# GpSimd takes half of the hidden-tile exchange, and VectorE's order around it is changed, in a two-layer decoder trunk

## The chip, the cores and the metric

The kernel runs on one core of one Trainium2 chip, all arithmetic in float32 (matmuls on split operands, below). The metric is the device time of one execution in microseconds. Three runs of the kernel before gave 2172.32, 2172.74 and 2172.97 us; the median is 2172.74 us.

## What is computed

A trunk of two layers over 256 tokens with 2048 features. Layer 0 mixes with a recurrent unit and dilated attention, layer 1 with differential attention; each mixer is followed by a layer norm, then by an MLP with a squared ReLU (2048 to 8192 to 2048) and a second layer norm. The change touches the MLPs alone, so the mixers are left out here.

```python
D_MODEL = 2048; SEQ = 256; DEPTH = 2; D_FF = 4 * D_MODEL

def layer_norm(x, g, b):
    xf = x.astype(jnp.float32)
    mu = jnp.mean(xf, axis=-1, keepdims=True)
    var = jnp.mean(jnp.square(xf - mu), axis=-1, keepdims=True)
    y = (xf - mu) * lax.rsqrt(var + LN_EPS) * g.astype(jnp.float32) + b.astype(jnp.float32)
    return y.astype(x.dtype)

def squared_relu_mlp(x, w1, w2):
    h = jax.nn.relu(x @ w1)
    return (h * h) @ w2

def reference(x, positions, ev_w_in, ev_conv_w, ev_conv_b, ev_gate_a_w, ev_gate_a_b, ev_gate_x_w,
              ev_gate_x_b, ev_rg_lambda, ev_w_out, od_w_in, od_lambda_q1, od_lambda_k1, od_lambda_q2,
              od_lambda_k2, od_subln_g, od_w_out, ln_mix_g, ln_mix_b, ln_mlp_g, ln_mlp_b, mlp_w1, mlp_w2):
    cos, sin = rope_tables(positions)
    for layer in range(DEPTH):
        p = layer // 2
        if layer % 2 == 0:
            mix = even_mixer(x, cos, sin, ev_w_in[p], ev_conv_w[p], ev_conv_b[p], ev_gate_a_w[p], ev_gate_a_b[p],
                             ev_gate_x_w[p], ev_gate_x_b[p], ev_rg_lambda[p], ev_w_out[p])
        else:
            lambda_init = 0.8 - 0.6 * math.exp(-0.3 * layer)
            mix = odd_mixer(x, cos, sin, od_w_in[p], od_lambda_q1[p], od_lambda_k1[p], od_lambda_q2[p],
                            od_lambda_k2[p], od_subln_g[p], od_w_out[p], lambda_init)
        x = layer_norm(ALPHA * x + mix, ln_mix_g[layer], ln_mix_b[layer])
        x = layer_norm(ALPHA * x + squared_relu_mlp(x, mlp_w1[layer], mlp_w2[layer]), ln_mlp_g[layer], ln_mlp_b[layer])
    return x
```

## The kernel before

**Split operands.** Each float32 weight chunk is loaded into `raw`, ScalarE copies it rounded into `w_hi` (`split_hi`), and VectorE writes the rest into `w_lo` (`split_lo`, L1005). The activations are split in the same way. A product is three matmuls: hi by hi, hi by lo, lo by hi (L714 to L716). A chunk is 2 x 128 rows by 512 columns of a weight, and a natural chunk is 12 matmuls of 128x512. Eight chunks are one block. `raw` has eight places, loaded in pairs by SP; `w_hi` and `w_lo` have four, so ScalarE splits chunk k when TensorE has used chunk k - 4.

**The MLP.** It is worked in 16 blocks of 512 hidden features (`FB`). For each there is an "up" block of eight chunks (x times w1 into PSUM banks 0 and 1) and a "down" block of eight chunks (hidden times w2 into banks 4 to 7, added into `res`). The up block of the first 512 features stands in `lead`; then iteration i of `up_down` does the up block i + 1 and the down block i: 16 chunks. On VectorE and ScalarE an iteration is the loop `for k in range(2, 18)`: chunk k of 2 to 7 belongs to the up block, 8 to 15 to the down block, and 16 and 17 to the next iteration. Chunks 0 and 1 are split in the iteration before. Iteration 0 (`first=True` on VectorE) and iteration 14 (`last=True`) are written out, 1 to 13 are a hardware loop. The down block of the last 512 features follows.

**The exchange.** The up product has tokens on partitions, the down product needs hidden features there. VectorE transposes the 32x32 squares out of PSUM into `cross` (`blocks_turned`, L1403, at k = 9), and 16 DMAs then move whole squares between the four groups of 32 partitions, from `cross` (`tiles_turned`) to `ks` (`tiles_moved`), 32 KB each (`move_hidden`, L301, on SP's queue). SP issues them behind the load of the first pair of the down block (`down`, L304) and ahead of its other pairs. Then VectorE takes the squared ReLU from `ks` into `qs` (`squared`, L1410, at k = 4), ScalarE copies its rounded part into `yT` (`hidden_hi`, L587, at k = 5), and VectorE writes the rest (`hidden_lo`, L1416, at k = 5). TensorE waits for `hidden_lo` ahead of the down block. In iteration 14 the exchange of the last block follows its transpose at once: a second `squared` comes at k = 12 and a second `hidden_lo` at k = 13.

**Other work of VectorE there.** `add_down` (L1077) adds the four down products into the residual at k = 11, 13, 15 and 17. In iteration 0 alone, `gain_residual` (L1068 and L1071) multiplies the residual by gain and ALPHA and adds the bias, one of four column groups at k = 6, 8, 12 and 14. `add_down` of a group waits for its scaling.

**GpSimd** issues the loads of gain and bias for the four layer norms (L359). Each waits until the four scalings with the values before have been made (`s_gained`). At the end it works on parts of the last layer norm. SP, GpSimd and the engines run their own instructions in order; a wait blocks all that is behind it on that engine.

Of the kernel before, what the change touches and what calls it, by code (L numbers as in the profile page):

```python
# [69 lines left out]
FB = D_FF // CN  # L70
# [74 lines left out]
def build(nc, x, positions, ev_w_in, ev_conv_w, ev_conv_b, ev_gate_a_w, ev_gate_a_b, ev_gate_x_w,  # L145
# [11 lines left out]
    with ExitStack() as ctx:  # L157
# [3 lines left out]
        def sem(name):  # L161
# [73 lines left out]
        s_bn, s_k8, s_var, s_std, s_shift = (  # L235
            sem("block_statistics"), sem("softplus_made"), sem("variance"),
            sem("std"), sem("shift"))
        s_block_tr, s_moved = sem("hidden_blocks_turned"), sem("hidden_blocks_moved")
        s_sq, s_hhi, s_hlo = sem("hidden_squared"), sem("hidden_hi"), sem("hidden_lo")
        s_S, s_neg, s_exp, s_P, s_T, s_pT, s_O = (sem("scores"), sem("neg_max"), sem("exps"), sem("probs"),  # L240
                                                  sem("probs_turned"), sem("probs_turned_copied"),
# [26 lines left out]
        @block.sync  # L268
        def _(sp):
            def load(blk, q, src):  # L270

                sp.wait_ge(s_lo, (blk - 1) * BLK + (2 * q + 2))
                sp.dma_start(raw[:, 2 * q:2 * q + 2].rearrange("p k t c -> p (k t) c"), src).then_inc(s_raw[q], 16)

            xv = x[0].rearrange("(t p) n -> p t n", p=P)
            sp.dma_start(cst[:, 0:P], consts[:, 0:P]).then_inc(s_id, 16)
            for k in range(BLK):
                cols = slice(k * CK * P, (k + 1) * CK * P)
                sp.dma_start(res[:, :, cols], xv[:, :, cols]).then_inc(s_x[k], 16)
                first = w_ein[k // 2, EVEN_IN_COLS[0]][:, k % 2 * CK:k % 2 * CK + CK]  # L280
                sp.dma_start(raw[:, k], first).then_inc(s_first[k], 16)
            sp.dma_start(cst[:, P:K_W], consts[:, P:K_W]).then_inc(s_cst, 16)
            for b, col in enumerate(EVEN_IN_COLS[1:], 1):
                for q in range(PAIRS):
                    load(B_EIN + b, q, w_ein[q, col])

            def load_out(order, blk, w):
                for n, (nb, kp, _, _) in enumerate(order[::2]):
                    load(blk + n // PAIRS, n % PAIRS, w[kp // 2, nb])

            def mlp(layer, b0):
                def up(blk, b):
                    for q in range(PAIRS):
                        load(blk, q, w_m1[layer][q, b])

                def move_hidden(b):

                    sp.wait_ge(s_block_tr, b + (layer * FB + 1))
                    for a in range(NQ):
                        for c in range(NQ):  # L300
                            sp.dma_start(tiles_moved[QUAD * c:QUAD * c + QUAD, :, a],  # L301
                                         tiles_turned[QUAD * a:QUAD * a + QUAD, c]).then_inc(s_moved, 16)

                def down(blk, b):  # L304
                    for q in range(PAIRS):
                        load(blk, q, w_m2[layer][b, q])
                        if q == 0:
                            move_hidden(b)
                up(b0, 0)
                with sp.Fori(0, FB - 1) as i:  # L310
                    up(i * 2 + (b0 + 1), i + 1)
                    down(i * 2 + (b0 + 2), i)
                down(b0 + 2 * FB - 1, FB - 1)

            load_out(EVEN_OUT, B_EOUT, w_eout)
            mlp(0, B_M0)
            with sp.Fori(0, GROUPS) as g:
                for j in range(3):
                    for q in range(PAIRS):
                        load(g * 3 + (B_OIN + j), q, w_oin[q, g + j * (D // CN)])  # L320
            load_out(ODD_OUT, B_OOUT, w_oout)
            mlp(1, B_M1)
            ov = out[0].rearrange("(t p) n -> p t n", p=P)
            dve_1, dve_2, dve_3 = ((s_fin_dve, n + 1, *piece) for n, piece in enumerate(FIN_DVE))
            pool_1, pool_2, pool_3 = ((s_fin_pool, n + 1, *piece) for n, piece in enumerate(FIN_POOL))
            stores = (dve_1, pool_1, pool_2, dve_2, pool_3, dve_3)
            for ready, count, tok, a, b in stores:
                sp.wait_ge(ready, count)
                sp.dma_start(ov[:, tok, a:b], res[:, tok, a:b]).then_inc(s_out, 16)
            sp.wait_ge(s_out, 16 * len(stores))  # L330
# [3 lines left out]
        def _(pool):  # L334
# [15 lines left out]
                    pool.dma_start(gates_w[64 * half:64 * half + 64, n, :, 64 * half:64 * half + 64], src).then_inc(s_gw, 16)  # L350


            for n in range(4):
                if n == 0:
                    pool.wait_ge(s_yalo, 2)
                else:
                    pool.wait_ge(s_gained, GROUPS * n)
                for i, row in enumerate(ln_rows(n)):
                    pool.dma_start(gain_bias[:, i], row.partition_broadcast(P)[:, 0, :]).then_inc(s_gb, 16)  # L359
            pool.wait_ge(s_gb, 128)  # L360

            for n, (tok, a, b) in enumerate(FIN_POOL):
# [8 lines left out]
        def _(act):  # L371
# [209 lines left out]
            def mlp(n, b0):  # L581

                def hidden_hi(b, dst=hT):
                    act.wait_ge(s_sq, b + 1)
                    if dst is hT:
                        act.wait_ge(s_used, last_down(b))
                    nc.scalar.activation(dst[:, :, 0].rearrange("p f (n i) -> p f n i", i=QUAD), hidden,  # L587
                                         ACT.Copy).then_inc(s_hhi, 1)

                h0 = FB * (n // 2)  # L590
                def last_down(b):
                    return ((b - h0) * 2 + b0 + 1) * BLK
                lead(n + 1, b0)

                def up_down(i, last=False):

                    blk = i * 2 + (b0 + 1)
                    for k in range(2, 18):
                        split_hi(blk, k)
                        if k == 5:  # L600
                            hidden_hi(i + h0)
                        if k == 13 and last:
                            hidden_hi(i + h0 + 1, hT_last)

                with act.Fori(0, FB - 2) as i:
                    up_down(i)
                up_down(FB - 2, last=True)
                last = b0 + 2 * FB - 1
                for k in range(2, BLK):
                    split_hi(last, k)  # L610
                if last + 1 < B_END:
                    split_hi(last + 1, 0)
                    split_hi(last + 1, 1)
                layer_norm(n + 1)
# [384 lines left out]
        def _(dve):  # L999
# [397 lines left out]
            def mlp(n, b0, n0):  # L1397
# [8 lines left out]

                def squared(b):

                    dve.wait_ge(s_moved, (b + (h0 + 1)) * (16 * NQ * NQ))
                    nc.vector.scalar_tensor_tensor(out=flat(qs[:]), in0=flat(ks[:]), scalar=0.0, in1=flat(ks[:]),  # L1410
                                                   op0=ALU.max, op1=ALU.mult).then_inc(s_sq, 1)

# [12 lines left out]
                def up_down(i, last=False, first=False):  # L1425

                    blk = i * 2 + (b0 + 1)
                    for k in range(2, 18):
                        split_lo(blk, k)
                        if k == 4:  # L1430
                            squared(i)
                        if k == 5:
                            hidden_lo(i)
                        if k == 9:
                            blocks_turned(blk, 0)
                        if first and k in (6, 8, 12, 14):
                            gain_residual(n, (6, 8, 12, 14).index(k))
                        if k == 12 and last:
                            squared(i + 1)
                        if k == 13 and last:  # L1440
# [142 lines left out]
```

## Time and profile before

| | before |
|---|---|
| median of 3 runs | 2172.74 us (2172.32 to 2172.97) |
| the profiled execution | 2174.45 us |
| span of its profile | 2172.3 us |
| mean granted TensorE clock | 0.997 of full speed |
| first MLP, up and down blocks | about 350 to 1060 us |
| second MLP | about 1450 to 2160 us |
| VectorE, ScalarE busy | 65%, 45% of the span |
| GpSimd busy | 1% of the span |
| DMA engines | 59.5% of the 16 engines' span by SP's queue, 1.3% by GpSimd's |

The profile is one execution. "Busy" counts instructions on an engine; matmuls are pipelined, so a record is drawn longer than the step from one to the next. A wait is the idle time of an engine ahead of an instruction, put down to what released it last. A DMA issue is the time the issuing queue spends on it; its landing is counted from the start of the issue. Instructions of one kind that follow each other are shown as one row with their number behind an x.

### The profile page before, as it was taken

How to read it: one execution, taken by the hardware profiler on the slowest of the kernel's cores; microseconds unless marked ns; L12 is line 12 of the kernel's file. 1: busy time of each engine (PE TensorE's matmuls, PEld its weight loads, DVE VectorE, ACT ScalarE, POOL GpSimd, SP SyncE). 2: the span in 40 equal slices, each digit the busy share in tenths (PEclk: the TensorE clock that was granted, in tenths of full speed). 3: DMA queues.
4: the chain of work that ended last, by engine and by line, in shares of the span. 5: the costliest groups of instructions: out<-in, count | busy, mean ns of one | idle time of the engine just before them, and what ended most of it. 6: DMA issues, size and time to landing. Idle time of an engine off the chain costs nothing.

```text
span 2172.3 us, 27393 instructions
## 1 busy us (share of the span) xinstructions
PE 2135.4 (98%) x10034; PEld 1786.2 (82%) x10034; DVE 1418.1 (65%) x1448; ACT 983.6 (45%) x1160; POOL 28.5 (1%) x38
## 2 busy tenths in 40 slices
PE   8999999999999999999999999999999999999996
PEld 7888888788888888887888888887888888888885
DVE  5766766666656665666787666567666666666657
ACT  4445656344434444444645545554444444444442
POOL 2000000000000000000000000000000000000002
PEclk9999999999999999999999999999999999999999
DMA  8555565666666666665564555555766666666662
GB/s 279 175 175 158 178 241 161 211 217 209 203 192 215 211 203 192 212 213 190 180 214 157 191 173 174 175 164 179 244 207 210 203 201 206 210 201 203 206 207 103
DMA packets 244768, 425.83 MB, mean 196 GB/s; under 512 B 14993, under 2 KB 50049, under 8 KB 243697
## 3 DMA queue, kind: packets, MB, share of 16 engines
q1 hardware_dynamic: 242880, 415.75, 59.5%
q0 software_dynamic: 1840, 9.44, 1.3%
q8 instruction: 31, 0.51, 0.1%
q14 instruction: 17, 0.13, 0.0%
HBM read 406.26 MB, written 2.10 MB: 188 GB/s over the span
## 4 chain that ended last, share of the span: by engine, by line
PE 91%; DVE 4%; SPq 3%; DMA 1%; issue 1%; ACT 0%; DVEq 0%
PE ps L714 24%; PE ps L716 24%; PE ps L715 24%; PE ps L688 10%; PE ps L692 5%; SPq L301 3%; DVE w_lo L1005 1%; DMA raw<-in_ev_w_in 1%; DMA ks<-cross 1%; PE ps L789 0%; DVE res L1077 0%; PE ps L754 0%; PE ps L830 0%; DVE res L1068 0%; PE ps L734 0%
## 5 line engine op out<-in xcount | busy, mean ns | idle before, releaser
L380 ACT ACTIVATE w_hi<-raw 128x1024 fp32r<-128x1024 f32 x752 | 786.5, 1058 | 808.7 <-PE ps L716 747.9
L1005 DVE TENSOR_TENSOR w_lo<-raw,w_hi 128x1024 fp32r<-128x1024 f32 x752 | 895.5, 1217 | 163.9 <-ACT w_hi L380 163.6
L714 PE MATMUL ps<-w_hi,yT 128*128 128x512 f32 x1240 | 484.3, 391 | 4.1 <-DVE w_lo L1005 4.1
L714 PE MATMUL ps<-w_hi,xT 128*128 128x512 f32 x1216 | 476.4, 392 | 7.1 <-DVE w_lo L1005 4.9
L716 PE MATMUL ps<-w_hi,yT 128*128 128x512 f32 x1240 | 482.5, 389 | 0.0
L715 PE MATMUL ps<-w_lo,yT 128*128 128x512 f32 x1240 | 482.5, 389 | 0.0
L716 PE MATMUL ps<-w_hi,xT 128*128 128x512 f32 x1216 | 474.0, 390 | 0.0
L715 PE MATMUL ps<-w_lo,xT 128*128 128x512 f32 x1216 | 473.9, 390 | 0.0
L1077 DVE TENSOR_TENSOR res<-ps,res 128x1024 f32<-128x1024 f32 x131 | 160.3, 1223 | 219.3 <-PE ps L716 219.3
L714 PEld LDWEIGHTS ps<-w_hi,yT 128*128 128x128 f32 x1240 | 232.7, 188 | 53.9 <-DVE w_lo L1005 5.8
L714 PEld LDWEIGHTS ps<-w_hi,xT 128*128 128x128 f32 x1216 | 228.7, 188 | 56.8 <-DVE w_lo L1005 7.2
L716 PEld LDWEIGHTS ps<-w_hi,yT 128*128 128x128 f32 x1240 | 232.7, 188 | 48.4
L715 PEld LDWEIGHTS ps<-w_lo,yT 128*128 128x128 f32 x1240 | 232.8, 188 | 48.2
L716 PEld LDWEIGHTS ps<-w_hi,xT 128*128 128x128 f32 x1216 | 228.6, 188 | 47.9
L715 PEld LDWEIGHTS ps<-w_lo,xT 128*128 128x128 f32 x1216 | 228.7, 188 | 47.1
L688 PE MATMUL ps<-xT,w_hi 128*128 128x512 f32 x1024 | 261.9, 397 | 1.8 <-DVE xT L1035 1.5
L688 PEld LDWEIGHTS ps<-xT,w_hi 128*128 128x128 f32 x1024 | 185.0, 189 | 36.6 <-DVE xT L1035 2.0
L1410 DVE SCALAR_TENSOR_TENSOR qs<-ks 128x1024 f32<-128x1024 f32 x32 | 39.2, 1225 | 172.5 <-DMA ks<-cross 172.5
L692 PEld LDWEIGHTS ps<-xT,w_lo 128*128 128x128 f32 x1024 | 137.4, 190 | 9.6 <-DVE xT L1035 1.1
L692 PE MATMUL ps<-xT,w_lo 128*128 128x256 f32 x1024 | 143.7, 284 | 0.9 <-DVE xT L1035 0.9
L587 ACT ACTIVATE yT<-qs 128x1024 fp32r<-128x1024 f32 x32 | 34.0, 1061 | 171.5 <-DVE qs L1410 171.5
L1403 DVE STREAM_TRANSPOSE cross<-ps 128x1024 f32<-128x1024 f32 x32 | 40.0, 1249 | 92.7 <-PE ps L716 92.7
(181 smaller groups left out, 781.1 us busy)
## 6 DMA issues: line engine op xcount, KB each, us to landing
raw<-in_mlp_w SPq DMA_DIRECT2D x256, 1024.0 KB, 5.2
raw<-in_od_w_in SPq DMA_DIRECT2D x48, 1024.0 KB, 5.2
raw<-in_ev_w_in SPq DMA_DIRECT2D x36, 1024.0 KB, 5.1
raw<-in_ev_w_out SPq DMA_DIRECT2D x16, 1024.0 KB, 5.1
ks<-cross SPq DMA_DIRECT2D x512, 32.0 KB, 1.9
raw<-in_od_w_out SPq DMA_DIRECT2D x16, 1024.0 KB, 5.1
raw<-in_ev_w_in SPq DMA_DIRECT2D x8, 512.0 KB, 12.4
res<-in_x SPq DMA_DIRECT2D x8, 256.0 KB, 9.3
```

The source lines that it names most:

```text
L301: sp.dma_start(tiles_moved[QUAD * c:QUAD * c + QUAD, :, a], tiles_turned[QUAD * a:QUAD * a + QUAD, c]).then_inc(s_moved, 16)
L380: nc.scalar.activation(flat(w_hi[:, k % NSPL]), flat(raw[:, k % NRAW]), ACT.Copy).then_inc(s_hi, 1)
L587: nc.scalar.activation(dst[:, :, 0].rearrange("p f (n i) -> p f n i", i=QUAD), hidden, ACT.Copy).then_inc(s_hhi, 1)
L688: return nc.tensor.matmul(ps[:, f], w_hi[:, k % NSPL, i, f * P:f * P + P], both, start=k == 0 and i == 0, stop=k == BLK - 1 and i == CK - 1)
L692: return nc.tensor.matmul(ps[:, f, S:2 * S], w_lo[:, k % NSPL, i, f * P:f * P + P], xT[:, CK * k + i, 0], start=False, stop=False)
L714: nc.tensor.matmul(bank, src[:, kt + i, 0, toks], hi, start=(start and i == 0), stop=False)
L715: nc.tensor.matmul(bank, src[:, kt + i, 0, toks], lo, start=False, stop=False)
L716: ins = nc.tensor.matmul(bank, src[:, kt + i, 1, toks], hi, start=False, stop=(stop and i == CK - 1))
L1005: nc.vector.tensor_tensor(flat(w_lo[:, k % NSPL]), flat(raw[:, k % NRAW]), flat(w_hi[:, k % NSPL]).bitcast(F32), ALU.subtract).then_inc(s_ ...
L1077: nc.vector.tensor_tensor(res[:, :, nb * CN:nb * CN + CN], ps[:, pair[0]:pair[0] + 2], res[:, :, nb * CN:nb * CN + CN], ALU.add).then_inc( ...
L1403: nc.vector.transpose(tiles_turned.rearrange("p c t f i -> p (t f) c i"), ps[:, bank:bank + 2].rearrange("p t (f c j) -> p (t f) c j", c=N ...
L1410: nc.vector.scalar_tensor_tensor(out=flat(qs[:]), in0=flat(ks[:]), scalar=0.0, in1=flat(ks[:]), op0=ALU.max, op1=ALU.mult).then_inc(s_sq, 1)
```

## The change

Three edits. On GpSimd a function `move_hidden` is added: it waits for the transpose and issues the DMAs of the source groups a = 2 and 3, 8 of the 16, with a semaphore of their own; SP keeps a = 0 and 1. GpSimd does block 0 of an MLP behind the load of the mixer norm's gain and bias, and blocks 1 to 15 behind the load of the MLP norm's. `squared` waits for both semaphores. VectorE squares behind chunk 6 instead of 4 and writes the hidden tile's low part behind 7 instead of 5, ScalarE its high part behind 7 instead of 5. In iteration 0 the four scalings of the residual stand behind chunks 2, 3, 10 and 12 instead of 6, 8, 12 and 14.

```diff
--- before.py
+++ after.py
@@ -235,7 +235,8 @@
         s_bn, s_k8, s_var, s_std, s_shift = (
             sem("block_statistics"), sem("softplus_made"), sem("variance"),
             sem("std"), sem("shift"))
-        s_block_tr, s_moved = sem("hidden_blocks_turned"), sem("hidden_blocks_moved")
+        s_block_tr, s_moved, s_moved_pool = (sem("hidden_blocks_turned"), sem("hidden_blocks_moved"),
+                                          sem("hidden_blocks_moved_by_gpsimd"))
         s_sq, s_hhi, s_hlo = sem("hidden_squared"), sem("hidden_hi"), sem("hidden_lo")
         s_S, s_neg, s_exp, s_P, s_T, s_pT, s_O = (sem("scores"), sem("neg_max"), sem("exps"), sem("probs"),
                                                   sem("probs_turned"), sem("probs_turned_copied"),
@@ -296,7 +297,7 @@
                 def move_hidden(b):
 
                     sp.wait_ge(s_block_tr, b + (layer * FB + 1))
-                    for a in range(NQ):
+                    for a in range(NQ // 2):
                         for c in range(NQ):
                             sp.dma_start(tiles_moved[QUAD * c:QUAD * c + QUAD, :, a],
                                          tiles_turned[QUAD * a:QUAD * a + QUAD, c]).then_inc(s_moved, 16)
@@ -350,6 +351,14 @@
                     pool.dma_start(gates_w[64 * half:64 * half + 64, n, :, 64 * half:64 * half + 64], src).then_inc(s_gw, 16)
 
 
+            def move_hidden(count):
+
+                pool.wait_ge(s_block_tr, count)
+                for a in range(NQ // 2, NQ):
+                    for c in range(NQ):
+                        pool.dma_start(tiles_moved[QUAD * c:QUAD * c + QUAD, :, a],
+                                       tiles_turned[QUAD * a:QUAD * a + QUAD, c]).then_inc(s_moved_pool, 16)
+
             for n in range(4):
                 if n == 0:
                     pool.wait_ge(s_yalo, 2)
@@ -357,6 +366,11 @@
                     pool.wait_ge(s_gained, GROUPS * n)
                 for i, row in enumerate(ln_rows(n)):
                     pool.dma_start(gain_bias[:, i], row.partition_broadcast(P)[:, 0, :]).then_inc(s_gb, 16)
+                if n % 2 == 0:
+                    move_hidden(n // 2 * FB + 1)
+                else:
+                    for b in range(1, FB):
+                        move_hidden(b + (n // 2 * FB + 1))
             pool.wait_ge(s_gb, 128)
 
             for n, (tok, a, b) in enumerate(FIN_POOL):
@@ -597,7 +611,7 @@
                     blk = i * 2 + (b0 + 1)
                     for k in range(2, 18):
                         split_hi(blk, k)
-                        if k == 5:
+                        if k == 7:
                             hidden_hi(i + h0)
                         if k == 13 and last:
                             hidden_hi(i + h0 + 1, hT_last)
@@ -1406,7 +1420,8 @@
 
                 def squared(b):
 
-                    dve.wait_ge(s_moved, (b + (h0 + 1)) * (16 * NQ * NQ))
+                    dve.wait_ge(s_moved, (b + (h0 + 1)) * (8 * NQ * NQ))
+                    dve.wait_ge(s_moved_pool, (b + (h0 + 1)) * (8 * NQ * NQ))
                     nc.vector.scalar_tensor_tensor(out=flat(qs[:]), in0=flat(ks[:]), scalar=0.0, in1=flat(ks[:]),
                                                    op0=ALU.max, op1=ALU.mult).then_inc(s_sq, 1)
 
@@ -1427,14 +1442,14 @@
                     blk = i * 2 + (b0 + 1)
                     for k in range(2, 18):
                         split_lo(blk, k)
-                        if k == 4:
+                        if k == 6:
                             squared(i)
-                        if k == 5:
+                        if k == 7:
                             hidden_lo(i)
                         if k == 9:
                             blocks_turned(blk, 0)
-                        if first and k in (6, 8, 12, 14):
-                            gain_residual(n, (6, 8, 12, 14).index(k))
+                        if first and k in (2, 3, 10, 12):
+                            gain_residual(n, (2, 3, 10, 12).index(k))
                         if k == 12 and last:
                             squared(i + 1)
                         if k == 13 and last:
```

## Rows read from the trace of the kernel before

**Rows 1.** The page's first part: busy us of each engine, share, count.

```profile
PE 2135.4 (98%) x10034; PEld 1786.2 (82%) x10034; DVE 1418.1 (65%) x1448; ACT 983.6 (45%) x1160; POOL 28.5 (1%) x38
```

**Rows 2.** TensorE's waits, windows 340:480, 1000:1080, 1440:1560, 2090:2173: total, times, longest.

```profile
PE ps L714 <- DVE w_lo L1005: 3.0, 2, 2.8
...
PE ps L714 <- DVE w_lo L1005: 2.1, 2, 1.6
...
PE ps L714 <- DVE w_lo L1005: 1.9, 2, 1.6
...
PE ps L714 <- DVE w_lo L1005: 2.0, 2, 1.6
```

**Rows 3.** VectorE in order of time, middle iterations: start us, us, line, tiles, [idle before].

```profile
522.67 1.23 DVE L1410 SCALAR_TENSOR_TENSOR qs<-ks 128x1024 f32<-128x1024 f32 x1 [5.08 <-DMA ks<-cross]
...
534.31 1.25 DVE L1403 STREAM_TRANSPOSE cross<-ps 128x1024 f32<-128x1024 f32 x1 [3.12 <-PE ps L716]
...
577.83 1.25 DVE L1403 STREAM_TRANSPOSE cross<-ps 128x1024 f32<-128x1024 f32 x1 [3.12 <-PE ps L716]
```

**Rows 4.** TensorE in order of time, at two of its waits.

```profile
393.15 0.50 PE L714 MATMUL ps<-w_hi,xT 128*128 128x512 f32 x1 [2.82 <-DVE w_lo L1005]
...
397.13 0.39 PE L715 MATMUL ps<-w_lo,xT 128*128 128x512 f32 x1
...
1498.42 0.39 PE L716 MATMUL ps<-w_hi,xT 128*128 128x512 f32 x1
...
1498.94 0.50 PE L714 MATMUL ps<-w_hi,xT 128*128 128x512 f32 x1
```

**Rows 5.** The windows view, 394 to 398 us: busy us, PEclk, DMA share, GB/s.

```profile
394.00:398.00 4.00, 4.00 (x13) 3.17 (x12) 3.97 (x5) 2.11 (x4) 0.00 (x0) 0.63 0.79 275
```

**Rows 6.** VectorE in order of time, first iteration of the first MLP.

```profile
376.77 1.25 DVE L1403 STREAM_TRANSPOSE cross<-ps 128x1024 f32<-128x1024 f32 x1 [3.06 <-PE ps L716]
...
380.59 1.23 DVE L1005 TENSOR_TENSOR w_lo<-raw,w_hi 128x1024 fp32r<-128x1024 f32 x1 [0.32 <-ACT w_hi L380]
...
390.74 1.22 DVE L1410 SCALAR_TENSOR_TENSOR qs<-ks 128x1024 f32<-128x1024 f32 x1 [8.93 <-DMA ks<-cross]
...
416.81 1.22 DVE L1068 SCALAR_TENSOR_TENSOR res<-res,rg 128x1024 f32<-128x1024 f32 x1
...
418.06 1.23 DVE L1071 SCALAR_TENSOR_TENSOR res<-rg,res 128x1024 f32<-128x1024 f32 x1
```

**Rows 7.** SP's queue in order of time, issues of three exchanges.

```profile
378.05 11.43 SPq L301 DMA_DIRECT2D ks<-cross  x16
...
424.40 10.28 SPq L301 DMA_DIRECT2D ks<-cross  x16
...
1014.30 10.19 SPq L301 DMA_DIRECT2D ks<-cross  x16
```

**Rows 8.** The chain of work, last iteration: start us, us, what.

```profile
1023.90 1.87 DMA ks<-cross
```

**Rows 9.** VectorE in order of time, last iteration of the first MLP.

```profile
1013.02 1.25 DVE L1403 STREAM_TRANSPOSE cross<-ps 128x1024 f32<-128x1024 f32 x1 [3.06 <-PE ps L716]
...
1025.80 1.22 DVE L1410 SCALAR_TENSOR_TENSOR qs<-ks 128x1024 f32<-128x1024 f32 x1 [4.97 <-DMA ks<-cross]
...
1028.14 1.23 DVE L1416 TENSOR_TENSOR yT<-qs,yT 128x1024 fp32r<-128x1024 f32 x1
```

**Rows 10.** GpSimd in order of time: two DMA issues.

```profile
1.26 0.71 POOL L335 DMA_DIRECT2D rg<-in_positions  x1 [0.80 <-POOLq L1574]
...
419.58 0.53 POOL L359 DMA_DIRECT2D rg<-in_ln_mlp_g  x1 [124.60 <-DVE res L1071]
```

**Rows 11.** DMA issues from GpSimd: count, KB each, median us to landing.

```profile
late<-in_ev_gate_x_w POOLq DMA_DIRECT2D x2, 128.0 KB, 10.0
...
rg<-in_positions POOLq DMA_DIRECT2D x1, 32.0 KB, 3.5
...
rg<-in_ev_conv_w POOLq DMA_DIRECT2D x1, 16.0 KB, 5.1
```

## The prediction

> **What bounds the kernel now.** I read the busy shares first [rows 1]: TensorE is busy for 2135.4 of the span's 2172.3 us, so only what makes TensorE wait can be won. Next I read its waits, window by window [rows 2]. All of its waiting for split weights, 9.0 us, lies in four places, two waits in each: the first two iterations and the last iteration of `up_down` in the first MLP (3.0 and 2.1 us) and in the second (1.9 and 2.0 us). The 12 iterations between them in each MLP have none.
>
> A wait costs more than its bracket. One matmul of 128x512 starts every 0.227 us: one iteration is 192 of them and two transposes of successive iterations start at 534.31 and 577.83, so 43.52 / 192 [rows 3]. A record is drawn 0.39 us long, so the bracket leaves out 0.16 us, and the first matmul behind a wait lasts 0.50 instead of 0.39 [rows 4]. Each of the eight waits therefore costs its bracket and 0.27 us. In the first MLP the longest one does more. The granted clock falls: it is 0.63 on average from 394 to 398 us [rows 5], where matmuls run at 1.2 GHz for a while instead of 2.4. From 393.15 to 397.13 there are ten steps in 3.98 us instead of 2.27 [rows 4]; 0.11 of that is in my 0.27, so the clock takes 1.6 us. Finally the matmul at 1498.94 is 0.50 long with no bracket, so a wait too short to be listed: 0.4 us by the starts.
> Sum: 9.0 + 8 x 0.27 + 1.6 + 0.4 = **13.2 us**. Early iterations: (3.0 + 1.9) + 4 x 0.27 + 1.6 + 0.4 = 8.0. Last iterations: (2.1 + 2.0) + 4 x 0.27 = 5.2.
>
> **Why TensorE waits there.** In the first iteration VectorE splits chunk 4 at 380.59 and then stands in `squared`, waiting for the exchange, until 390.74 [rows 6]. Chunk k of the iteration is due at 376.77 + 2.72 k (12 matmuls a chunk; the transpose at 376.77 marks the end of the block before), so chunk 5 at 390.4, but it is split only behind `squared`, by 390.74 + 2 x 1.22 = 393.2. The exchange is 16 transfers that SP issues one behind the other in 11.43 us, or 10.19 us where there is no hiccup, so 0.64 us each [rows 7], and the last lands 1.87 us after its issue begins [rows 8]. The issuing is the long part, not the transfers. In the last iteration the second `squared` has the same shape: transpose at 1013.02, exchange landed at 1025.8, hidden_lo at 1028.14 [rows 9]. In a middle iteration SP issues before the iteration starts, and `squared` at 522.67 makes nobody late [rows 3].
>
> **The change, part by part.**
> *Order on VectorE and ScalarE.* `squared` goes from behind chunk 4 to behind chunk 6, the hi and lo of the hidden tile from behind 5 to behind 7. Nothing is added. What becomes late next: chunk 7, due at 376.77 + 19.04 = 395.8. `squared` and its split take 2 x 1.22, so the exchange may land as late as 393.4, 15.4 us after the transpose ended; even SP alone landed at 390.7. Chunk 8, due at 398.5, follows hidden_lo: 389.1 + 4 x 1.23 = 394, or 395.7 if the exchange landed at 390.7. So the order alone removes the wait of the first iteration, if the splits ahead of `squared` are in time. The small one of the second iteration goes too: its exchange is issued from 424.40 [rows 7] and lands by 436.5, and chunk 7 is due there at 420.3 + 19.0 = 439.3.
> They now share VectorE with two residual scalings (behind 2 and 3), each two instructions, 2.48 us from 416.81 to 419.29 [rows 6]. From 378.0: chunk 2 at 379.2, scaling 381.7, chunk 3 at 382.9 (due 384.9), scaling 385.4, chunk 4 at 386.6 (due 387.7), 5 at 387.8 (due 390.4), 6 at 389.1 (due 393.1). The least margin is 1.0 us. Second half, from the transpose that ends at 399.8: 10, scaling, 11 by 404.7 (due 406.7), an addition, 12 by 407.2 (due 409.4), scaling, 13 by 410.9 (due 412.1), an addition, 14 by 413.3 (due 414.9). No wait: **-8.0 us**. Before, four scalings fell in the backlog behind the late `squared`.
> *GpSimd takes 8 of the 16 transfers.* SP's 8 are issued in 5.1 instead of 10.2 us: last iteration 1014.3 + 7 x 0.64 + 1.9 = 1020.7. GpSimd waits for the transpose itself. It reacts in about 0.3 us (the scaling that releases it ends at 419.29, it issues at 419.58), and its issue takes 0.53 us, 0.71 where it moved 32 KB to 32 partitions [rows 10]. So the last issue begins at 1014.3 + 0.3 + 7 x 0.53 = 1018.3. The trace has no such transfer from GpSimd's queue. From below its landing is SP's own 1.9 us; from above 5.1 us (16 KB) and 10.0 us (gate weights), both while SP's first loads kept the DMA engines full [rows 11]. I take 3.5 us, the 32 KB transfer that was issued first of all, as the engines are nearly idle here too. Landed: 1021.8 (1020.2 to 1028.3), against 1025.8 now. Chunk 13 is due at 1013.0 + 5 x 2.72 = 1026.6; with `squared` and the split the exchange may land at 1024.2. Chunk 14, due at 1029.3, comes behind `squared`, split, hidden_lo, addition and split, 6 us: 1023.3. Both hold up to a landing of 5 us: **-5.2 us**.
> *Other things that the edit touches.* VectorE gets a second wait in `squared`, nothing where the engine idles there. SP's loads behind the exchange are issued 5 us earlier; they gate nobody now. On GpSimd the exchanges of blocks 1 to 15 stand behind the reload of gain and bias, which waits for the fourth scaling (409.6) and takes two issues; block 1's half is then issued by 415.3, and SP's half of it only begins at about 424. In middle iterations GpSimd issues right behind the transpose, and `squared` comes some 30 us later (534.31 to 522.67 + 43.52). `squared` on one queue's 8 transfers still waits for SP, whose half begins just before the iteration.
> Sum: -13.2 us against this execution's 2174.45 us (span 2172.3) gives 2161.2. The median of the runs is 1.7 us lower, 2172.74, so **2159.5 us**.
>
> *A rule against it.* The rows show 10.2 us of issuing for 512 KB and 1.9 us of landing [rows 7, 8]. The Trainium skill, DMA: Bandwidth & Descriptors, section Issuing engines are not separate DMA queues, says that several issuers only save the sequencer's issue time, usually small beside the DMA. Read as "does not help", it would leave the 5.2 us of the last iterations in place; the trace speaks for the reverse here, as issue time is five times the landing.
>
> **The rivals.**
> 1. *GpSimd's half lands as late as SP's whole did.* That takes a landing of 7.5 us: 14.3 + 0.3 + 3.7 + 7.5 = 25.8. For it: 5.1 and 10.0 us in [rows 11]. Against: full engines there, idle ones here. Only the order pays: 2172.74 - 8.0 = 2164.7. At 10.0 us each last iteration is 2.5 us worse than now: 2169.7, within 0.2%. Chance 0.12 for up to 2167, 0.06 for up to 2177.
> 2. *The exchange becomes longer, so slower.* Let x be the time from the end of the transpose to the last landing (now 11.5). The early iterations bear 15.4, the last ones 9.0 before the two delays count; the kernel is slower by 0.2% when 2 (x - 15.4) + 2 (x - 9.0) exceeds 13.2 + 4.4, so from x = 16.6, which is a GpSimd issue of 1.8 us instead of 0.53 (16.6 - 0.3 - 3.5, by 7). At 2.0 us it is x = 17.8, +22.4 - 13.2: 2181.9. Place: the first and last iterations; in the middle ones GpSimd's half has about 37 us. Against: 0.53 us at 419.58 was measured while VectorE split weights. Chance 0.07. The mechanism that would do it is a VectorE that keeps GpSimd from writing its descriptors; the Trainium skill, SBUF — State Buffer, section Who interferes with whom, has this for VectorE's two-port modes and not for `tensor_tensor`. No row here shows it.
> 3. *The scalings make chunk 4 or 13 late* (margins 1.0 and 1.2 us). Half a microsecond over in each of the two first iterations (one per MLP) costs 0.8 each with the 0.27: 2161.1. Chance 0.05. The same time comes out if the timed runs never had the slow clock.
> 4. *The edit does nothing*, as GpSimd's half waits for something else (a reload, a full ring): then rival 1.
>
> **Chances and range.** The forecast 2159.5 has 0.70. The range runs from 2158 (rounding of the waits) to 2167 (rival 1 half way to its bound). This kernel can be told from no change at about 0.2%, 4.3 us, so below 2168.4 is faster: 0.70 + 0.12 + 0.05 = 0.87; within: 0.06; slower: 0.07.
>
> **What would show it.** Right: TensorE waits for w_lo fall from eight to none or nearly; clock 1.0 at 394 to 398; the exchange from 378 landed by about 386, `squared` at about 389, and the transpose-to-`squared` time in the last iteration about 7.5 us instead of 11.5. Wrong: a GpSimd issue over 0.8 us, `squared` in the last iteration released by GpSimd's queue after 1024, or a new w_lo wait at chunks 3, 4 or 13 of the first iteration.

## The result, and the profile after

The changed kernel takes 2167.34 us (median of 8 runs, 2166.14 to 2169.22), the kernel before 2174.28 us on the same chip (8 runs, 2172.32 to 2176.41). The ratio is 0.9968, 95% interval 0.9958 to 0.9978: 6.9 us or 0.32% faster. The forecast was 13.2 us. The sign held and half of the size was missing. The time also lay just above the range, 2167.34 against 2167.0. Of the 7.8 us between it and the forecast of 2159.5, 1.5 are the base: the prediction started from 2172.74, and the kernel before, run beside the changed one, had 2174.28. From the prediction's own base the ratio gives 2165.8, inside the range. The other 6.3 us are gain that did not come, and they are what has to be explained.

The profiled execution took 2168.23 us (span 2166.1; before 2174.45 and 2172.3). I first read where TensorE waits, over the whole span: engine, line, waited for, us in total, times, longest.

```profile
PE ps L768 <- DMA res<-in_x: 7.3, 3, 5.0
PE ps L768 <- DVE res L1130: 2.6, 3, 0.9
PE ps L728 <- DVE xT L1049: 2.1, 2, 1.0
PE ps L702 <- DVE xT L1049: 1.7, 2, 1.0
PE ps L706 <- DVE xT L1049: 0.6, 1, 0.6
```

No line for w_lo is left, where there were eight waits and 9.0 us [rows 2]. The slow clock is gone with them. Here are the two windows around chunk 7 (us, then busy us of PE, PEld, DVE, ACT, POOL, then PEclk, DMA share, GB/s), to be held against [rows 5]:

```profile
390.00:394.00 4.00, 4.00 (x20) 3.30 (x19) 3.90 (x4) 2.10 (x3) 0.00 (x0) 1.00 0.97 310
394.00:398.00 4.00, 4.00 (x19) 3.32 (x18) 1.23 (x1) 2.03 (x2) 0.00 (x0) 1.00 0.70 229
```

VectorE in its first iteration, in order of time (start us, us, line, tiles, [idle before]), against [rows 6]:

```profile
377.59 1.25 DVE L1417 STREAM_TRANSPOSE cross<-ps 128x1024 f32<-128x1024 f32 x1 [3.06 <-PE ps L730]
...
385.79 3.49 DVE L1019 TENSOR_TENSOR w_lo<-raw,w_hi 128x1024 fp32r<-128x1024 f32 x3
389.19 1.22 DVE L1425 SCALAR_TENSOR_TENSOR qs<-ks 128x1024 f32<-128x1024 f32 x1
...
391.54 1.23 DVE L1431 TENSOR_TENSOR yT<-qs,yT 128x1024 fp32r<-128x1024 f32 x1
```

`squared` starts 11.6 us after the transpose and without idle time; before it was 14.0 us, 8.9 of them idle. In the last iteration VectorE, GpSimd and SP (three views in order of time, put under each other) stand like this, against [rows 7] and [rows 9]:

```profile
1008.62 1.25 DVE L1417 STREAM_TRANSPOSE cross<-ps 128x1024 f32<-128x1024 f32 x1 [3.06 <-PE ps L730]
...
1016.34 1.22 DVE L1425 SCALAR_TENSOR_TENSOR qs<-ks 128x1024 f32<-128x1024 f32 x1
```

```profile
1010.37 2.10 POOL L359 DMA_DIRECT2D ks<-cross  x4 [39.44 <-DVE cross L1417]
1012.65 2.11 POOL L359 DMA_DIRECT2D ks<-cross  x4 [0.18 <-issue]
```

```profile
1009.90 5.09 SPq L302 DMA_DIRECT2D ks<-cross  x8
```

From transpose to `squared` it is 7.7 us, where it was 12.8. Both halves are issued by 1015.0. Over the kernel GpSimd's issue is 0.53 us and its landing 1.9 us; these are its line's own view (durations in ns) and the row of the DMA issues (count, KB each, median us to landing):

```profile
L359 POOL DMA_DIRECT2D ks<-cross x256: 533/533/574, 379.1 to 2107.1; - x128
...
DMA to landing us min/median/max: 1.7/1.9/8.1
```

```profile
ks<-cross POOLq DMA_DIRECT2D x256, 32.0 KB, 1.9
```

So the middle of the kernel did what was forecast. Then the rest must lie at the end. The last instruction of VectorE, before and after:

```profile
2167.53 1.63 DVE L1125 SCALAR_TENSOR_TENSOR res<-res,tiny,rg 128x512 f32<-128x512 f32 x1
```

```profile
2154.88 1.63 DVE L1139 SCALAR_TENSOR_TENSOR res<-res,tiny,rg 128x512 f32<-128x512 f32 x1
```

The work ends 12.65 us earlier, the span only 6.2 us. Behind the last operation each engine's queue ends with a drain and a barrier that all must reach. The chain of waits stops at VectorE's last operation and does not show them; they show when the line on which they stand, L157, is asked for. Columns: queue, instruction, duration in ns min/median/max, start of the first and the last. Before:

```profile
L157 POOLq DRAIN  x1: 3914/3914/3914, 2167.0 to 2167.0; - x1
L157 DVEq DRAIN  x1: 1670/1670/1670, 2167.5 to 2167.5; - x1
L157 SPq DRAIN  x1: 7/7/7, 2172.1 to 2172.1; - x1
```

After:

```profile
L157 POOLq DRAIN  x1: 11518/11518/11518, 2154.3 to 2154.3; - x1
L157 DVEq DRAIN  x1: 1672/1672/1672, 2154.9 to 2154.9; - x1
L157 SPq DRAIN  x1: 7/7/7, 2159.5 to 2159.5; - x1
```

And the barrier behind them, which every engine passes at 2166.0, when GpSimd has come:

```profile
L157 POOLq EVENT_SEMAPHORE  x2: 17/17/17, 2165.9 to 2166.0; - x2
L157 SPq EVENT_SEMAPHORE  x1: 17/17/17, 2166.0 to 2166.0; - x1
L157 DVEq EVENT_SEMAPHORE  x1: 21/21/21, 2166.0 to 2166.0; - x1
```

SP reaches its drain when the output stores have landed. Before, that was last (2172.1) and GpSimd's drain had ended at 2167.0 + 3.9 = 2170.9, 1.2 us ahead. After, the stores are in at 2159.5 and GpSimd's drain ends at 2154.3 + 11.5 = 2165.8, 6.3 us behind them. The drain is 7.6 us longer, 1.2 of it still hidden.

For the comparisons below I cut each profiled execution into two pieces. The **body** runs from the first transpose of the first MLP to SP's drain, so it leaves out the start, which is up to 3.6 us longer in one execution than in another (the first transpose comes at 376.74 to 380.35). The **tail** runs from SP's drain to the end of the span. Before: 2172.1 - 376.77 = 1795.3 and 0.2. After: 2159.5 - 377.59 = 1781.9 and 6.6. So the body lost 13.4 us and the tail gained 6.4.

### The profile page after: what moved, and what is told of

The parts are those of the page before. It is cut to its first block, busy times and chain, and to the rows that moved or that the text cites. A ratio compares the mean times of both kernels' runs of the same rounds, so it can differ in the third digit from the quotient of the medians.

```text
span 2166.1 us, 27425 instructions
## 1 busy us (share of the span) xinstructions
PE 2130.8 (98%) x10034; PEld 1785.7 (82%) x10034; DVE 1423.9 (66%) x1448; ACT 990.6 (46%) x1160; POOL 163.6 (8%) x294
## 4 chain that ended last, share of the span: by engine, by line
PE 96%; DVE 1%; DMA 1%; ACT 0%; SPq 0%; issue 0%
PE ps L728 26%; PE ps L730 26%; PE ps L729 26%; PE ps L702 10%; PE ps L706 5%; DMA raw<-in_ev_w_in 1%; PE ps L803 0%; PE ps L768 0%; PE ps L844 0%; PE ps L748 0%; PE ps L747 0%; PE ps L746 0%; PE ps L802 0%; PE ps L807 0%; DVE res L1139 0%; DVE stats L1105 0%
## 5 line engine op out<-in xcount | busy, mean ns | idle before, releaser
L359 POOL DMA_DIRECT2D ks<-cross x256 | 135.0, 536 | 1513.8 <-DVE cross L1417 1510.5
```

The costliest lines, as they stand in the source:

```text
L359: pool.dma_start(tiles_moved[QUAD * c:QUAD * c + QUAD, :, a], tiles_turned[QUAD * a:QUAD * a + QUAD, c]).then_inc(s_moved_pool, 16)
```

## The experiments

The theory after the result: the two edits on the path are worth 13.2 us as forecast, and GpSimd's closing drain, which grows with the transfers that GpSimd has issued, gives 6.4 back. The rivals: the order alone is worth all and the split nothing or less, and GpSimd's late end has another cause than its transfers. The kernels of one group ran on one chip with the kernel before beside them. The cuts of code leave out what only follows from an edit: the declarations, and the numbers for which `squared` waits on each queue.

### The parts alone, and two ways around the drain

`e1_order_only`: the new order, SP issues all 16 (against the changed kernel).

```
-                    for a in range(NQ // 2):
+                    for a in range(NQ):
...
-                if n % 2 == 0:
-                    move_hidden(n // 2 * FB + 1)
-                else:
-                    for b in range(1, FB):
-                        move_hidden(b + (n // 2 * FB + 1))
```

> SP issues all 16 transfers as before; only the order on VectorE and ScalarE and the places of the four scalings are those of the changed kernel. Theory A (all waits went as forecast, and the missing part is a longer drain of GpSimd at the end, 11.5 us instead of 3.9, caused by the transfers that GpSimd issued): the early waits go (8.0 us), the last iterations keep 5.2 us, GpSimd's drain stays at 3.9 us; 8.0 us faster than before, so within 1 us of the changed kernel. Theory B (the drain is long for another reason, not GpSimd's transfers): the drain is 11.5 us here too, and the kernel is about as fast as before (0 to 1 us).

Measured: 2166.89 us (5 runs) against 2175.74 (15 runs): 0.9957 (0.9943 to 0.9970), 8.85 us faster. `squared` stands at 394.21, 13.9 us after its transpose at 380.35, and idles 2.16 us for the exchange; TensorE waits for w_lo only in the last iterations:

```profile
PE ps L714 <- DVE w_lo L1005: 4.2, 4, 1.6
```

The body is 2167.7 - 380.35 = 1787.3, 8.0 less than before. The tail is 0.2. The forecast's 8.0 for the order holds. But the whole changed kernel, 6.9 us faster than its own kernel before, is no better than this part of it.

`e2_split_only`: GpSimd's half, the old order.

```
-                        if k == 7:
+                        if k == 5:
...
-                        if k == 6:
+                        if k == 4:
...
-                        if first and k in (2, 3, 10, 12):
+                        if first and k in (6, 8, 12, 14):
```

> GpSimd issues half, but VectorE and ScalarE keep the order of before. Theory A: the exchange lands 7 us behind the transpose instead of 11.5, so chunk 5 of the first iteration is split by 387.7 (due 390.4) and no wait of more than 0.3 us is left anywhere: 13 us less on TensorE, 7.6 us more drain, 5 to 6 us faster than before, like the changed kernel; the new order is then worth nothing beside the split. Rival: the order carries the early iterations, their 8 us stay, and only the 5.2 us of the last ones go: 2 us slower than before with the drain.

Measured: 2171.15 us (11 runs), 0.9978 (0.9969 to 0.9987), 4.6 us faster. Body 2163.0 - 377.92 = 1785.1, 10.2 less than before; tail 6.6. Two waits for w_lo are left, 1.8 us, where I expected none over 0.3 us, and most of that (1.4) has a cause of its own: in the second MLP's first iteration GpSimd's issue stops for 2.6 us between the sixth and the seventh transfer.

```profile
1473.41 3.22 POOL L359 DMA_DIRECT2D ks<-cross  x6 [347.70 <-DVE cross L1417]
1479.24 1.06 POOL L359 DMA_DIRECT2D ks<-cross  x2 [2.60 <-issue]
```

So the two edits overlap: 8.0 and 10.2 alone, 13.4 together. The order is what makes that stop harmless. The changed kernel has the same stop (2.61 us at 1478.21), and its `squared` idles 0.85 us there and makes nobody late.

`e3_last_only`: the new order; GpSimd issues its half only for the last block of each MLP, 16 transfers instead of 256.

```
-                    for a in range(NQ // 2):
+                    for a in range(NQ // 2 if isinstance(b, int) and b == FB - 1 else NQ):
...
+                if n % 2 == 1:
+                    move_hidden((n // 2 + 1) * FB)
```

> New order; GpSimd issues half only of the last block's exchange in each MLP, 16 transfers instead of 256; SP issues the rest. Theory A1 (each transfer issued by GpSimd adds 0.03 us to its last drain, 7.6 us for 256): all 13.2 us of waits gone, drain 4.4 us, 12.7 us faster than before, 2161.5 us. Theory A2 (the longer drain is a fixed price of late or many-partition transfers on that queue): drain 11.5 us, 5.6 us faster than before.

Measured: 2162.12 us (5 runs), 0.9936 (0.9922 to 0.9949), 13.6 us faster. No wait for w_lo; body 2158.7 - 376.74 = 1782.0, tail 0.3:

```profile
L157 POOLq DRAIN  x1: 5232/5232/5232, 2153.6 to 2153.6; - x1
L157 SPq DRAIN  x1: 7/7/7, 2158.7 to 2158.7; - x1
```

The drain ends at 2158.8, together with the stores. All of the body's gain comes from 16 of the 256 transfers and the order; the other 240 only lengthen the drain.

`e4_early_drain`: the changed kernel, and GpSimd drains once behind the last exchange, where it idles for 36 us.

```
                         move_hidden(b + (n // 2 * FB + 1))
+            nc.gpsimd.drain()
             pool.wait_ge(s_gb, 128)
```

> The changed kernel with one more drain instruction on GpSimd behind its last exchange, some 36 us before it has other work. Theory C1 (the drain works off a backlog once): the early drain takes 8 to 12 us in idle time, the last one falls back to 2 to 4 us, and the kernel is 13 us faster than before, 2161 us. Theory C2 (each drain costs by all that was ever issued, or the cost is not of the drain instruction itself): the last drain stays at 11.5 us and the time is that of the changed kernel.

Measured: 2162.08 us (5 runs), 0.9938 (0.9924 to 0.9951), 13.7 us faster. The early drain took 10.5 us at 2107.3 in idle time, and of the closing one 1.7 us are left:

```profile
L374 POOLq DRAIN  x1: 10480/10480/10480, 2107.3 to 2107.3; - x1
```

```profile
L157 POOLq DRAIN  x1: 1697/1697/1697, 2154.6 to 2154.6; - x1
L157 SPq DRAIN  x1: 7/7/7, 2159.7 to 2159.7; - x1
```

Body 1782.0, tail 0.2. The transfers are the same 256; the only thing that changed is when the drain is paid for. This settles that the missing half was the drain's. (The early drain's record begins 0.6 us before GpSimd's last issue ends, so 9.9 us of it are the drain alone.)

### What the drain grows with

GpSimd's last operation starts at the same time as the closing drain and lasts 1.6 us (L381, 2154.37). The drain without it is what the table below counts, and of an early drain the part behind the last issue.

`e5_quarter`: GpSimd takes only a = 3, 4 of 16, in all blocks.

```
-                    for a in range(NQ // 2):
+                    for a in range(NQ - 1):
...
-                for a in range(NQ // 2, NQ):
+                for a in range(NQ - 1, NQ):
```

> GpSimd issues a quarter of each exchange (group a = 3), 128 transfers in all, SP 12 of 16. With its own 27 that makes 155 on its queue. So far the last drain was 3.9 us at 27, 5.2 at 43 and 11.5 at 283; each holds 1.6 us of GpSimd's last operation. Theory D1 (0.085 us a transfer up to a ceiling of about 9.9 us, reached near 117 transfers): 11.5 us here. Theory D2 (a fixed jump and 0.026 us a transfer): 8.1 us. Theory D3 (by bytes or descriptors, with curvature): between 8 and 10. TensorE: SP's 12 issues land 7.7 + 1.9 = 9.6 us behind the transpose, 0.6 us over the 9.0 that the last iterations bear, so one wait of 0.2 to 0.6 us in each of them.

Measured, one run: 2165.13 us (before: 2175.17, 9 runs). The drain was 6.6 us, so 5.0 without the last operation, which none of the three expectations had; body 1782.2, tail 1.7, and no wait for w_lo where I expected 0.2 to 0.6 us.

`e6_tiny64`: the kernel before with 64 transfers of 32 bytes, each into one partition, that GpSimd issues in the second iteration of the first MLP; nothing needs them.

```
+                if n == 1:
+                    for m in range(64):
+                        pool.dma_start(spare[m:m + 1], consts[m:m + 1, 0:8]).then_inc(s_spare, 16)
+                    pool.wait_ge(s_spare, 1024)
```

> The kernel before, and in the middle of the first MLP 64 more transfers from GpSimd of 32 bytes to one partition each, which nothing needs: 91 on its queue. If a transfer costs the drain the same whatever its size (0.085 us): drain 9.3 us. If it goes by bytes or by descriptors: drain 4 to 5 us. TensorE's waits as before, 9.0 us; the span grows only by what the drain reaches beyond the last store.

Measured, one run: 2184.17 us (before: 2175.17).

```profile
L157 POOLq DRAIN  x1: 9143/9143/9143, 2172.7 to 2172.7; - x1
L157 SPq DRAIN  x1: 7/7/7, 2177.9 to 2177.9; - x1
```

The drain is 5.2 us longer for 64 transfers, 0.082 us each, as the count had it: 32 bytes cost as much as 32 KB. The tail is 4.2. The body is 4.8 us longer too, which I had not expected: in the second iteration, where the tiny transfers are issued beside the exchange, TensorE's wait for w_lo is 3.3 us instead of 0.2, and the clock behind it is 0.73 between 444 and 448 us.

```profile
421.57 31.51 POOL L363 DMA_DIRECT2D spare<-consts  x64
```

`e7_first_mlp`: GpSimd's half in the first MLP only, 128 transfers, the last of them 1100 us before the end.

```
-                if n % 2 == 0:
+                if n == 0:
...
-                else:
+                elif n == 1:
```

> GpSimd issues half of the exchanges in the first MLP alone, 128 transfers, the last of them 1100 us before the end; SP issues all 16 in the second MLP. New order everywhere. If the drain goes by what was issued since the start, however long ago: as the quarter kernel, which has the same count. If it goes by recent or unfinished transfers: 3.9 us. TensorE: the waits of the first MLP gone, the 2.6 us of the second MLP's last iteration stay.

Measured, one run: 2171.65 us (before: 2175.17). Body 2162.6 - 378.00 = 1784.6, 10.7 less than before: the second MLP's last iteration keeps its wait (2.1 us, two times), half of the 5.2. The tail is 6.9:

```profile
L157 POOLq DRAIN  x1: 11843/11843/11843, 2157.4 to 2157.4; - x1
```

Transfers that landed more than 1100 us ago still lengthen the drain, so it does not wait for their data. The expectation had the drain of `e5_quarter`, which has the same count; it is 10.2 us without the last operation, against 5.0 there.

`e9_drain_midway`: the changed kernel with a drain behind block 8 of the second MLP, so that 56 transfers follow.

```
+                        if n == 3 and b == FB // 2:
+                            nc.gpsimd.drain()
```

> The changed kernel with one more drain on GpSimd behind block 8's exchange of the second MLP; 56 transfers follow it. Theory C1 (a drain works off the transfers issued since the one before, 0.082 us each): the last drain is 56 x 0.082 + 1.6 = 6.2 us, it ends 1.1 us behind the last store instead of 6.4, and the kernel is about 5 us faster than the changed one. If the last drain goes by all transfers ever issued, or by those of the whole second MLP: 11 us.

Measured, one run: 2164.17 us (before: 2173.76, 9 runs); the closing drain was 6.3 us, as expected, and the tail 1.3 us instead of 6.6. The drain in the middle stands behind 227 transfers (27 + 128 + 72). Its record begins before the last issue ends (1804.2) and ends 7.3 us behind it:

```profile
L375 POOLq DRAIN  x1: 8247/8247/8247, 1803.2 to 1803.2; - x1
```

`e10_last_only_drain` is `e3_last_only` with an early drain as in `e4_early_drain`.

> GpSimd in the last block's exchange alone, and an early drain as well. In the version without it the drain ended at 2158.8 and SP's wait for the stores at 2158.7 us. If the stores set the end: last drain 1.7 us and the same time within 0.3 us, 13.5 us faster than before. If the drain set it alone: up to 3 us faster than the version with GpSimd only in the last block.

Measured: 2162.14 us (5 runs) against 2173.76 (9 runs), 0.9947 (0.9934 to 0.9961). The closing drain fell to 1.7 us and the time stayed that of `e3_last_only`: in `e10_last_only_drain` the stores landed last, in `e3_last_only` they and the drain ended within 0.1 us. The early drain stands behind 43 transfers and ends 3.6 us behind the last issue (2107.5):

```profile
L371 POOLq DRAIN  x1: 4530/4530/4530, 2106.6 to 2106.6; - x1
```

| drain | GpSimd's transfers since the start or its last drain | us, less the work beside it | per transfer |
|---|---|---|---|
| closing, `e4_early_drain`, `e10_last_only_drain` | 0 | 0.1 us | |
| closing, before and `e1_order_only` | 27 | 2.3 us | 0.085 us |
| closing, `e3_last_only` | 43 | 3.6 us | 0.084 us |
| early, `e10_last_only_drain` | 43 | 3.6 us | 0.083 us |
| closing, `e9_drain_midway` | 56 | 4.7 us | 0.084 us |
| closing, `e6_tiny64` | 91 | 7.5 us | 0.083 us |
| closing, `e7_first_mlp` | 155 | 10.2 us | 0.066 us |
| closing, `e5_quarter` | 155 | 5.0 us | 0.032 us |
| in the middle, `e9_drain_midway` | 227 | 7.3 us | 0.032 us |
| closing, changed and `e2_split_only` | 283 | 9.9 us | 0.035 us |
| early, `e4_early_drain` | 283 | 9.9 us | 0.035 us |

An early drain takes as long as the closing one with the same transfers behind it (43: 3.6 and 3.6; 283: 9.9 and 9.9), so GpSimd's work at the end has no part in it. Up to 91 the drain is 0.083 us for each transfer. Above, it is less than the count, and not by the count alone: 155 transfers gave 10.2 us in one pattern and 5.0 in another.

One reading would be that GpSimd works off its backlog during the run, in the stop of 2.6 us: that one follows transfer 159 of the changed kernel, which leaves 283 - 159 = 124 behind it, and 124 x 0.083 is 10.3 against 9.9 measured. The other rows speak against it. The drain in the middle of `e9_drain_midway` has 68 transfers behind the same stop, so 5.6 us, and took 7.3. `e7_first_mlp` has no stop over 0.3 us and is still 2.6 us below 155 x 0.083. `e5_quarter` stops too: behind transfer 147 it begins the next exchange 1.9 us later than the rhythm of its blocks (43.5 us) has it, and the 8 transfers that follow would be 0.7 us, where 5.0 were measured.

```profile
2018.26 2.10 POOL L359 DMA_DIRECT2D ks<-cross  x4 [41.60 <-DVE cross L1417]
2063.46 2.11 POOL L359 DMA_DIRECT2D ks<-cross  x4 [43.10 <-issue]
```

What decides the drain above some hundred transfers stays open.

### Another queue than GpSimd's

`e8_scalar_queue`: ScalarE's queue issues the second half, behind its split of chunk 11; for block 0 of each MLP SP issues all 16. GpSimd issues no exchange.

```
+                    act.wait_ge(s_block_tr, count)
+                    for a in range(NQ // 2, NQ):
+                        for c in range(NQ):
+                            act.dma_start(tiles_moved[QUAD * c:QUAD * c + QUAD, :, a],
+                                          tiles_turned[QUAD * a:QUAD * a + QUAD, c]).then_inc(s_moved_pool, 16)
...
                             hidden_hi(i + h0)
+                        if k == 11:
+                            move_hidden(i + (h0 + 2))
```

> New order; the second half of each exchange but the first of each MLP is issued by ScalarE's queue, behind its 11th split, and not by GpSimd. Theory A (the long drain belongs to transfers from GpSimd): drain 3.9 us, all eight waits gone, as ScalarE has 4 us to spare there: 12 to 13.5 us faster than before, like the version with GpSimd only in the last block. Rival: 8 issues of 0.6 us on ScalarE delay splits 12 and 13 by up to 4 us in each of 30 blocks, chunk 12 is late by 0 to 1 us each time, and the kernel is up to 20 us slower than that version.

Measured: 2161.3 us (5 runs) against 2175.17 (9 runs), 0.9936 (0.9922 to 0.9950), 13.9 us faster. Body 1782.0, tail 0.2. ScalarE in order of time, last iteration:

```profile
1008.92 1.06 ACT L383 ACTIVATE w_hi<-raw 128x1024 fp32r<-128x1024 f32 x1 [1.66 <-PE ps L729]
1010.14 5.47 ACTq L598 DMA_DIRECT2D ks<-cross  x8
1015.72 2.01 ACT L383 ACTIVATE w_hi<-raw 128x1024 fp32r<-128x1024 f32 x2 [5.73 <-issue]
```

Eight issues take 5.47 us, 0.68 each, and hold up ScalarE's split of chunk 12 that long; VectorE then idles 1.28 us for it, and TensorE waits for no w_lo anywhere, so the rival did not come. ScalarE's closing drain stays at 0.8 us, GpSimd's at 3.9. What it costs is busy time of an engine with 45% of the span in use, and it costs nothing here.

## Why the prediction was wrong in size

**What held.** The price of the waits: 13.2 us forecast, and the body lost 13.4. The early iterations: 8.0 forecast, `e1_order_only` lost 8.0 in its body. The last iterations: 5.2 forecast, and 13.4 - 8.0 = 5.4. The order on VectorE: `squared` at 389.19 against 389.1 forecast (this execution's transpose was 0.8 us later), with its scalings behind chunks 2 and 3 and no late chunk, so rival 3 did not come. GpSimd's issue of 0.53 us held beside VectorE's work (533 at the least, 574 ns at the most), so rival 2 did not come. And the exchange took 5.1 us of issuing, as forecast. In the last iteration `squared` starts 6.5 us behind the end of its transpose; the forecast was 7.5, from 11.5, with the longer landing of the next paragraph. Rival 4 came in one place only: GpSimd's issue stopped for 2.6 us in the second MLP, and the new order bore it. What stops it no run shows.

**A term on the safe side.** I took 3.5 us for the landing of GpSimd's transfers, from a load at the kernel's start. It was 1.9 us, SP's own; the low bound was right, and a transfer at the kernel's start was no row for one in its middle. Both values clear the deadline of 5 us, so nothing followed from it. Rival 1 fell with it. The Trainium skill, DMA: Bandwidth & Descriptors, section Anatomy of one DMA — SWDGE (gpsimd) path, would have had it nearer: its 2.0 us and the size over 436 KB/us make an estimate of 2.1 us.

**The rule that I weighed.** The Trainium skill, DMA: Bandwidth & Descriptors, section Issuing engines are not separate DMA queues, says that several issuers only save issue time, and that is what they did here. The saving is the whole of the 5.4 us, since 10.2 us of issuing stood before 1.9 us of landing; "usually small" does not hold for 16 transfers of 32 KB behind each other.

**The step that failed.** It is the paragraph on other things that the edit touches, and with it the sum. I made the sum at TensorE, took the way from its last product to the end of the span for fixed, and asked of GpSimd only what its issues and waits cost. What stands behind the last operation on GpSimd's queue I never looked at, though the trace of before has it: a drain of 3.9 us on an engine that then had 38 instructions, ending 1.2 us ahead of the stores. That 1.2 us was all the cover there was, and I put 256 transfers on that queue. It cost 7.6 us, 6.4 of them in the open: 13.4 - 6.4 = 7.0, against 6.9 measured. None of the rivals was about the end of the program, so the range did not hold it either. What the trace of before could not give was the slope, 0.083 us for a transfer; with 27 transfers in 2.3 us as the only row, it would have given 0.085 x 256 = 21.8 us as an upper bound, and so a slower kernel as a serious rival.

The Trainium skill, VectorE: DVE Perf Modes, section The DRAIN you can't avoid, tells of drains that the runtime puts around a program, some 12 ns each on all engines. The drains at the start of this trace are like that on four engines (7 to 10 ns; GpSimd's is 182 ns, beside its first memsets). The closing ones stand on a line of the kernel, L157, where its instruction block is left, so they need not be those of the page, and its figure is no price for them. Only SP's, 7 ns, is near it. ScalarE's and VectorE's, 0.8 and 1.7 us, are as long as their last operations (0.81 and 1.63 us), TensorE's is 4.3 us in every run, and GpSimd's was 0.1 to 10.2 us without its last operation.

## What to carry to other kernels

Read the end of the program as well as its middle: list each engine's closing drain and which of them ends last, because an engine that is busy for 8% of the span can still hold the last barrier. When transfers are moved to GpSimd's queue, move only those whose issue time stands in somebody's way (here 16 of 256 gave all of the gain), or drain GpSimd in idle time before its last work, or use the queue of another engine with room. And when two edits remove the same wait, cost them alone and together: here 8.0 and 10.2 us make 13.4.

The best versions, `e3_last_only`, `e4_early_drain` and `e8_scalar_queue`, are 0.6% faster than before and cannot be told apart from each other. Each against its own kernel before, they gain 13.6 to 13.9 us where the changed kernel gains 6.9; the profiles' body and tail put the difference at 6.2 to 6.3 us.

## What the runs showed of the hardware

- GpSimd's closing drain takes 0.083 us for each transfer that GpSimd has issued since its last drain (27 to 91 transfers), whatever the size (32 bytes or 32 KB) and however long ago it landed. Above, no rule was found: 155 transfers gave 5.0 and 10.2 us, 227 gave 7.3, 283 gave 9.9. A drain behind the last issue clears it: 9.9 us for 283 transfers, 0.1 us left later.
- GpSimd's issue of such a transfer is 0.53 us, SP's 0.64, ScalarE's 0.68; GpSimd's lands after 1.9 us, like SP's in the kernel before.
- Where SP issues only 8 of the 16 in all blocks, the median landing of SP's transfers is 3.1 us (3.2 with ScalarE's queue, 2.4 with 12 of 16) instead of 1.9. TensorE waits for none of them; the cause is open.
- In the kernel before, TensorE's granted clock fell to 0.63 between 394 and 398 us, after TensorE had stood 2.8 us for w_lo. In `e6_tiny64` it fell twice, to 0.62 between 394 and 398 after a wait of 2.7 us and to 0.73 between 444 and 448 after one of 3.3. Behind the waits of at most 1.6 us in the other iterations it stayed at 1.00 in both, and in the changed kernel it is 1.00 through the first MLP, the 2.4 GHz level.
